# A two-block network on one core: expert e of the routed layer always in block e, six weight slots filled ahead, and the down product one block later

## The reference, cut to what matters

```
expert_id = grp[:, None] * EXPERTS_PER_GROUP + top_e          # 512 tokens x 2 = 1024 assignments
...
def run_block(args):
    xb, e, wb = args
    a = jax.nn.silu(xb @ w_gate[e]) * (xb @ w_up[e])           # 1024 -> 256, twice
    return (a @ w_down[e]) * wb[:, None].astype(xb.dtype)      # 256 -> 1024
```

## Time and profile before

| | |
|---|---|
| median of 3 runs | 1865.17 us (1861.14 to 1869.01) |
| the profiled execution, own time | 1860.19 us |
| its span | 1858.3 us |
| PE busy | 1615.7 us (87%) |
| DVE, POOL, ACT busy | 840.0, 499.6, 450.7 us |
| moved by DMA | 274.97 MB, mean 148 GB/s |
| mean granted TensorE clock | 0.927 of 2.4 GHz |

### The profile page before, as it was taken

One profiled execution on the slowest core, in us unless ns is written; L12 is line 12 of the kernel. 1 busy time (PEld: TensorE's weight loads), 2 busy tenths in 40 slices (PEclk: granted clock), 3 DMA queues, 4 the chain that ended last, 5 costly groups with the idle time before them and its releaser, 6 DMA issues.

```text
span 1858.3 us, 25135 instructions
## 1 busy us (share of the span) xinstructions
PE 1615.7 (87%) x9839; PEld 1303.2 (70%) x9839; DVE 840.0 (45%) x1469; ACT 450.7 (24%) x702; POOL 499.6 (27%) x208
## 2 busy tenths in 40 slices
PE   6967999998999999979999899899998578778782
PEld 5956676697989898958998787655888344444440
DVE  2344545528888884249208502464132523223234
ACT  4211232414222222233323323332232100000001
POOL 2450211123444443323432243200332011101103
PEclk9977999899999999979999999899999579998986
DMA  5161101032444452313221122200230399999994
GB/s 204 69 254 63 46 26 43 11 126 92 187 174 185 178 202 82 107 46 114 101 88 46 46 91 93 96 1 4 101 127 34 117 356 372 374 369 375 379 377 162
DMA packets 41435, 274.97 MB, mean 148 GB/s; under 512 B 5248, under 2 KB 5760, under 8 KB 17536
## 3 DMA queue, kind: packets, MB, share of 16 engines
q1 hardware_dynamic: 31872, 251.13, 36.1%
q0 software_dynamic: 4032, 13.63, 2.3%
q10 hardware_dynamic: 5440, 8.92, 1.3%
HBM read 250.07 MB, written 23.59 MB: 147 GB/s over the span
## 4 chain that ended last, share of the span: by engine, by line
PE 72%; DMA 13%; DVE 9%; ACT 3%; issue 2%; POOL 1%; ACTq 0%; SPq 0%; POOLq 0%; DVEq 0%
PE G L1719 18%; PE G L1721 17%; PE G L1720 17%; DMA wgu<-in_wexp_dram 9%; PE SA L1844 2%; PE SA L2200 2%; DMA arena<-in_wexp_dram 2%; PE G L1741 2%; PE OB L1863 2%; PE G L2200 1%; PE SA L2088 1%; PE PB L1853 1%; PE OB L2104 1%; PE OB L2215 1%; PE SA L2087 1%
## 5 line engine op out<-in xcount | busy, mean ns | idle before, releaser
L596 POOL TENSOR_TENSOR wl<-raw,wh 128x2048 fp32r<-128x2048 f32 x91 | 422.1, 4639 | 832.4 <-ACT wh L709 832.4
L709 ACT ACTIVATE wh<-raw 128x2048 fp32r<-128x2048 f32 x91 | 173.9, 1911 | 275.4 <-PE G L1721 273.2
L1719 PE MATMUL G<-Hh,wh 128*128 128x512 f32 x544 | 220.7, 406 | 4.7 <-DVE Yl L1526 1.6
L1719 PE MATMUL G<-wh,Yh 128*128 128x256 f32 (+2 forms) x700 | 206.3, 295 | 13.4 <-DVE arena L1463 7.3
L1721 PE MATMUL G<-Hh,wl 128*128 128x512 f32 x544 | 213.9, 393 | 0.0
L1720 PE MATMUL G<-Hl,wh 128*128 128x512 f32 x544 | 213.7, 393 | 0.0
L1721 PE MATMUL G<-wh,Yl 128*128 128x256 f32 (+2 forms) x700 | 204.3, 292 | 0.0
L1720 PE MATMUL G<-wl,Yh 128*128 128x256 f32 (+2 forms) x700 | 204.1, 292 | 0.0
L1719 PE MATMUL G<-wh,Hh 128*128 128x256 f32 x640 | 187.4, 293 | 2.6 <-DVE Hl L1530 2.1
L1720 PE MATMUL G<-wl,Hh 128*128 128x256 f32 x640 | 182.6, 285 | 0.0
L1721 PE MATMUL G<-wh,Hl 128*128 128x256 f32 x640 | 182.6, 285 | 0.0
(11 more groups left out here) (367 smaller groups left out, 2391.3 us busy)
## 6 DMA issues: line engine op xcount, KB each, us to landing
raw<-in_pieces_dram SPq DMA_DIRECT2D x91, 1024.0 KB, 4.9
arena<-in_wexp_dram SPq DMA_DIRECT2D x18, 2048.0 KB, 35.0
wgu<-in_wexp_dram SPq DMA_DIRECT2D x16, 2048.0 KB, 34.8
arena<-in_pieces_dram SPq DMA_DIRECT2D x24, 1024.0 KB, 4.8
arena<-in_wexp_dram SPq DMA_DIRECT2D x18, 1024.0 KB, 33.2
wdn<-in_wexp_dram SPq DMA_DIRECT2D x16, 1024.0 KB, 33.7
y_rows<-yb ACTq DMA_DIRECT2D x68, 128.0 KB, 8.9
y_rows<-arena SPq DMA_DIRECT2D x4, 2048.0 KB, 17.9
```

The lines of the kernel that those rows point to most:

```text
L596: pool.tensor_tensor(wl[:, split_slot(s)], wait_raw(pool, p), wh[:, split_slot(s)].bitcast(F32), ALU.subtract).then_inc(S("low_split"), 1)
L709: act.activation(wh[:, split_slot(s)], wait_raw(act, sp_list[s]), ACT.Copy).then_inc(S("high_split"), 1)
L1719: pe.matmul(out, ah, bh, start=first, stop=False)
```

## The change

1. **Order of blocks.** Block e (0 to 31) is always expert e, full or not. An expert's rows beyond 64 go to overflow blocks 32 and up (`OVER` = 16 at most), and only these stay in a loop with table and `If`. The first 32 blocks are written out on every engine. For the inputs here 34 blocks hold rows before; after, there are 32 and two overflow blocks.
2. **Weights.** Six slots in place of four. They are in memory that the earlier stages give up one after the other, and SP fills them as each is free: expert 0 ahead of piece `ga` 2, expert 1 and down of 2 behind the last piece, gate/up of 2 and 3 when the last `wout` product is done, the rest behind the store of `xn_rows` and the routing product. From then on gate/up of b+6 waits for `up_ready` of block b, down of b+6 for `y_ready` of b.
3. **Order on PE.** Down of b-1 follows gate/up of b. Rows are gathered four blocks ahead and turned two ahead. All four XT, GU, AB and YB banks alternate as before.
4. **Small things.** Routing has four more DVE operations (own block's first row). POOL uses the table directly for the first blocks, without a copy of the index. `final_g` is loaded later, in a slot. Two fills of `y_rows` in the first block's attention fall away (two of four 2 MB transfers).

The diff, cut to its core:

```
-NBLK = 48
-MIN_BLK = 2 * T // BS
+OVER = 16
+NBLK = NE + OVER
+AHEAD = 4
+NSLOT = 6
...
-        wgu = [AR(0, 2 * PIECE), AR(2 * PIECE, 2 * PIECE), wgu2[:, :], wgu3[:, :]]
-        wdn = [AR(4 * PIECE, PIECE), AR(5 * PIECE, PIECE), wdn2[:, :], wdn3[:, :]]
+        wgu = [AR(3 * PIECE, 2 * PIECE), gu_y[:, :], gu_w[0][:, :], gu_w[1][:, :], AR(PIECE, 2 * PIECE), gu_h[:, :]]
+        wdn = [AR(5 * PIECE, PIECE), dn_y[0][:, :], dn_y[1][:, :], AR(0, PIECE), dn_h[:, :], dn_l[:, :]]
...
+                if p == ("ga", 2):
+
+                    sp.wait_ge(S("scores_ready"), A0 + len(aunits))
+                    sp.wait_ge(S("score_biased"), A0 + len(aunits))
+                    expert_gu(0)
+                    expert_dn(0)
...
-            sp.dma_start(tab3, tab3_d).then_inc(S("tab3_loaded"), 16)
+            sp.dma_start(tab3, tab3_d[:, 0:TAB3_N]).then_inc(S("tab3_loaded"), 16)
+            expert_gu(1)
+            expert_dn(1)
+            expert_dn(2)
+            wait_group(sp, "wout", 7)
+            expert_gu(2)
+            expert_gu(3)
             sp.wait_ge(S("rows_normed"), 4 * NT)
             sp.dma_start(xn_rows.rearrange("(t p) n -> p t n", p=P), hraw3).then_inc(S("xn_stored"), 16)
             sp.wait_ge(S("xn_stored"), 16)
+            wait_group(sp, "h3", KT - 1)
+            wait_freed(sp, "wout", 7)
+            expert_gu(4)
+            expert_dn(3)
+            wait_group(sp, "gr", 0)
+            expert_dn(4)
+            expert_gu(5)
+            expert_dn(5)
+            for b in range(NE - NSLOT):
+                sp.wait_ge(S("up_ready"), b + 1)
+                expert_gu(b + NSLOT)
+                sp.wait_ge(S("y_ready"), b + 1)
+                expert_dn(b + NSLOT)
...
+            own(dve.tensor_tensor(own64, cols(tab3, TAB3, "iota_b")[:, 0:NE], ps64, ALU.subtract))
+            own(dve.tensor_scalar(Tmp, Sl, float(BS), None, ALU.is_lt))
+            own(dve.tensor_tensor(Tmp, Tmp, own64.unsqueeze(1).to_broadcast([P, NT, 32]), ALU.mult))
+            own(dve.tensor_tensor(Sl, Sl, Tmp, ALU.add))
...
+            for b in range(NE):
+                if b >= 2:
+                    dve.wait_ge(S("act_turned"), b - 1)
+                gated(b, b % 2)
+                scale_shift(b + 2, b % 2)
+                if b >= 1:
+                    row_out(b - 1)
...
+            def turn_and_down(b):
+
+                pe.wait_ge(S("act_whole"), b + 1)
+                if b >= 2:
+                    pe.wait_ge(S("act_copied"), b - 1)
+                act_turned(b % 2, pe.transpose)
+                if b + 3 < NE + 2:
+                    rows_of(b + 3)
+                pe.wait_ge(S(f"down_loaded{b % NSLOT}"), slot_count(b))
+                pe.wait_ge(S("act_copied"), b + 1)
+                if b >= 2:
+                    pe.wait_ge(S("y_copied"), b - 1)
+                down(b, b % 2, b % NSLOT)
...
+            rows_of(0)
+            rows_of(1)
+            for b in range(NE):
+                pe.wait_ge(S("xgT_ready"), b + 1)
+                pe.wait_ge(S(f"gu_loaded{b % NSLOT}"), slot_count(b))
+                if b >= 2:
+                    pe.wait_ge(S("act_whole"), b - 1)
+                gate_up(b, b % 2, b % NSLOT)
+                if b == 0:
+                    rows_of(2)
+                else:
+                    turn_and_down(b - 1)
+            turn_and_down(NE - 1)
```

More of the change, by code:

```diff
@@ L993, in _, with turned_copy, store @@
             act.activation(e2, m2, ACT.Exp).then_inc(S("second_exp"), 1)
+            def turned_copy(b):
+                act.wait_ge(S("act_turned"), b + 1)
+                if b >= 2:
+                    act.wait_ge(S("y_ready"), b - 1)
+                act.activation(actf[:, b % 2, :], AB[b % 2][:, 0:2 * BS], ACT.Copy).then_inc(S("act_copied"), 1)
+            def store(b):
+                act.wait_ge(S("y_copied"), b + 1)
+                for half in range(2):
+                    act.dma_start(y_rows[b * BS:(b + 1) * BS, half * 512:(half + 1) * 512], yb[BS * half:BS * half + BS, b % 2, :]).then_inc(S(f"y_stored{b % 2}"), 16)
@@ new lines, in _ @@
+            for b in range(NE):
+                if b >= 1:
+                    turned_copy(b - 1)
+                act.wait_ge(S("up_ready"), b + 1)
+                if b >= 2:
+                    act.wait_ge(S("tanh_free"), b - 1)
+                act.activation(tanhg[:, b % 2, :], GU[b % 2][0:BS, 0:256], ACT.Tanh, scale=0.5).then_inc(S("tanh_ready"), 1)
+                if b >= 2:
+                    store(b - 2)
+            turned_copy(NE - 1)
+            for b in (NE - 2, NE - 1):
+                store(b)
@@ new lines, in _ @@
+            row_out(NE - 1)
+            dve.wait_ge(S("bexp_ready"), 1)
+            blocks = dve.value_load(nblk_i[0:1, :], min_val=0, max_val=OVER)
+            with dve.Fori(0, OVER // WS) as i:
+                for v in range(WS):
+                    b, u = NE + WS * i + v, v % 2
+                    with dve.If(WS * i + v < blocks):
+                        dve.wait_ge(S("act_turned"), b - 1)
+                        gated(b, u)
+                        scale_shift(b + 2, u)
+                        dve.wait_ge(S("y_ready"), b + 1)
+                        dve.wait_ge(S(f"y_stored{u}"), 32 * (NE // 2) + 64 * i + 32 * (v // 2))
@@ L2169, in _, with gate_up @@
             pe.wait_ge(S("slot_idx_ready"), 1)
[L2172 to L2179 removed]
+            def gate_up(b, u, s):
+                wg = wgu[s].rearrange("p (j k n) -> p j k n", j=2, k=KT)
+                for k in range(KT):
+                    for j in range(2):
+                        ins = pe.matmul(GU[u][BS * j:BS * j + BS, 0:256], xgT[:, u, k, :], wg[:, j, k, :], start=k == 0, stop=k == KT - 1)
+                ins.then_inc(S("up_ready"), 1)
@@ L2180, in rows_transposed, with down, rows_turned @@
+            def down(b, u, s):
+                wd = wdn[s].rearrange("p (k n) -> p k n", k=2)
+                for k in range(2):
+                    for half in range(2):
+                        ins = pe.matmul(YB[u][BS * half:BS * half + BS, :], actf[:, u, k * BS:(k + 1) * BS], wd[:, k, half * 512:(half + 1) * 512],
+                                        start=k == 0, stop=k == 1)
+                ins.then_inc(S("y_ready"), 1)
+            def rows_turned(u, v, first):
                 for k in range(KT):
@@ L2211, in _ @@
-                        pe.wait_ge(S("act_copied"), b + 5)
-                        pe.wait_ge(S("y_copied"), b + 3)
-                        for k in range(2):
-                            for half in range(2):
-                                ins = pe.matmul(YB[u][BS * half:BS * half + BS, :], actf[:, u, k * BS:(k + 1) * BS], wd[:, k, half * 512:(half + 1) * 512],
-                                                start=k == 0, stop=k == 1)
-                        ins.then_inc(S("y_ready"), 1)
+                        pe.wait_ge(S(f"gu_loaded{s}"), before + 16 * i + 16)
@@ L2221, in _kxn @@
+                        pe.wait_ge(S("act_copied"), b + 1)
+                        pe.wait_ge(S("y_copied"), b - 1)
+                        down(b, u, s)
 def _kxn(w):
```

213 lines of the change are left out of this document (117 added, 96 removed).

## The result

The changed kernel took 1818.97 us (median of 4, 1814.19 to 1821.06) beside 1863.16 us (4 runs, 1858.84 to 1869.01) for the kernel before: ratio 0.976 [0.972, 0.979], 44 us faster. The profiled execution took 1820.64 us, 39.6 less than the profiled one of before and 8 less than the 1828.7 that the sum gave for it. So the direction and the place of the gain were right, and the size was not: the time lies 3 us under the range's low end.

What follows compares the result with a forecast made beforehand. DMA bytes at 374 GB/s were taken as the bound: 1498 + 281 + 3.5 = 1782.5 against 1814, so 31.5 us off 1860.2 gives 1828.7. The median forecast was 1831, range 1822 to 1845 (8 in 10).

Steps and rivals of the forecast that it cites:

- the sum: Whole kernel, profiled execution: 1860.2 us before, less 31.5 us for the earlier end of DMA, gives 1828.7.
- the rate of the full queue: Expert stage after the restart: 105.1 million bytes at the old kernel's 374 GB/s take 281.0 us; bounds 372 to 377.
- the restart: Start of expert blocks: expert 6's gate/up weights issued at 1496.7, transfer starting by 1498; bounds 1495 to 1500.
- the hole: After the restart, engines idle some 3.5 us while down weights of expert 6 wait for block 0; bounds 0 and 7.
- sixth step: In the chain to the restart: block 0's gathered rows land at 1487.2, 4.7 us after the gather at 1482.5.
- The tail: After the end of DMA: unchanged, since overflow blocks run in the old order with the same gathers and norm.
- Rival A: Expert stage: DMA stays the bound and about 31 us go; chance 0.79.
- B: Expert stage: PE becomes the bound through its lower clock, from 8.6 us a block; chance 0.07, of which 0.02 slower.
- D: Straight expert blocks: instructions arrive late, gain 12 or kernel 57 us slower; sign: idle PE without releaser; chance 0.05.
- the first 15 blocks or so: Sign of being right: PE has no wait for weights in these expert blocks, then one in each.
- C: Ahead of and entering the experts: piece `ga` 2 or `xn_rows` comes late, gain 15 to 25 us; chance 0.06.
- E: Expert stage: the queue is slower than before, at 356 GB/s, gain 17 us; chance 0.03.

Runs made afterwards that it cites:

- e7: Kernel before the change, with each gather held back by one added POOL wait until stores start, same bytes: 1851.99 us, ratio 0.995 to before.
- e13: Changed kernel with eight idle POOL products ahead of each gather of blocks 4 to 31, so it is issued after the stores: 1826.16 us, ratio 0.984.
- e4: Changed kernel with gathers of blocks 4 to 31 fetching 2 rows in place of 64: 1780.58 us, ratio 0.957 to the kernel before.
- e6: Changed kernel with a third result buffer for block 31 alone, run without the changed kernel beside it: 1815.65 us, ratio 0.977.
- e10: Changed kernel with gathers issued two blocks at a time and a third result buffer for block 31: 1820.15 us, ratio 0.979.
- e11: Same kernel as e6, run beside the changed kernel on one chip: 1815.58 us, ratio 0.975 to the kernel before.
- e3: Changed kernel with no expert loaded early; the six are issued when the block table is ready: 1856.02 us, ratio 0.999.
- e2: Changed kernel with the old order within a block, down and stores directly behind gate/up of the same block: 1818.71 us, ratio 0.979.
- e8: Changed kernel run again unaltered, as base on another chip: 1825.35 us, ratio 0.981 to the kernel before.
- e5: Kernel before the change with loop gathers of blocks 2 and up fetching 2 rows in place of 64: 1835.41 us, ratio 0.986.

## Why the prediction was wrong in size

**The failed step is the rate of the full queue.** "105.1 million bytes, 281.0 us" took 374 GB/s over from the old kernel, and I bounded it at 372 to 377. It measured 389 over 1510 to 1760, and the three profiled executions of the changed kernel have 384 to 389. From the restart (1494.96 and the 1.3 us that I had put behind the issue, so 1496.3; the first packet starts at 1495.93) to the end at 1769.3, less some 0.5 of hole, it is 272.5 us for the same bytes (the trace has 105.4 million), 8.5 less. The unchanged bytes, queue and share were no ground to keep it: the change moved the gathers to the stores, and the diff and a timeline of any later block would have told me to look at when the two are issued. That moving the gather to the stores raises the rate is shown by e7, without a byte changed: up by 20 GB/s and 9 us of time, clear of noise. e13, the way back, has the rate 6 GB/s lower and the time not clear of noise, so it agrees and proves little. e4 shows what gathers cost at all. e7 also moved the gather against the weight transfers, and why a gather costs less beside a store is not settled.

**The restart and the hole.** 1.7 and about 3 us early. The chain was right to its sixth step (rows there at 1487.1, forecast 1487.2). Its products were sized too long: 5.04, 3.67 and 1.94 us where I took 6.4, 4.5 and 3. The upper of the two clock levels is granted from 1492.7 on, behind 2.8 us of gate/up at the lower one, and nothing waits between the products.

**The tail "is the same"** was wrong by 5 us the other way. I followed the overflow blocks, which keep the old order, and not the last straight blocks, whose stores now come two blocks late. e6, e10 and e11 take that wait away, and their ends are some 3 to 8 us shorter in the traces, which is about these 5.

Together: 1.7 + 3 + 8.5 - 5.1 = 8.1 us, the whole difference between 1828.7 and 1820.6. The median is 12 under the forecast 1831: these 8, the 2.3 that I had put on the sum because the median of before stood above its profiled execution, and 1.7 by which the median of the changed kernel stands under its own. The range ended at 38 us of gain, and here a sum was off too: its own bounds (restart 1495, no hole, 105.1 million bytes at 377) give an end at 1773.8, 40 us of gain, and 24.5 at the other end. With 40 the profiled execution, 39.6 faster, lies just inside, but by luck: the longer tail hides 5 us of what the rate gave. The rate, the largest term, was bounded at 377 by rows of one kernel alone; with 384 to 389 the range would have held the result.

**What held.** The early transfers are issued as the order showed and cost nothing that can be told from the runs (`xn_rows` goes at 1440.98, 1.7 us later than before, but in e3, without them, it goes at 1442.18). Rival A was the case: share 1.02 in the stage, and the byte count with the rate of 389 gives an end at 1496.3 + 0.5 + 270.2 = 1767.0, 2 us before the one measured, since it ran slower at first (264 GB/s from 1500 to 1505). PE's block is 6.1 us at the upper level and 9.4 us are there for it (3.67 million bytes at 389), so B was farther off than I thought, though the clock of the 250 us is 0.89. The waits of PE in them:

```profile
PE SA L2280 <- issue: 27.4, 8, 3.7
PE G L2280 <- issue: 8.3, 3, 3.6
PE SA L2280 <- DVE arena L1745: 4.8, 2, 3.4
```

"issue" without a releaser was my sign for D, code that comes late, and 12 instruction packets fell into these 250 us. But e4 has the same straight code with 14 such packets, and its rows for the same 250 us are

```profile
PE SA L2284 <- issue: 3.9, 3, 1.9
PE G L2284 <- issue: 3.4, 1, 3.4
```

With less in the queue 28 of 36 us go away. The packets settle it: from block 11 to block 31 every gate/up of the changed kernel starts 0.5 to 1.1 us after the end of the last packet of its weights, so these waits are for weights whose landing the profile does not name, and D did not happen. (Up to block 10 the weights are in before PE asks for them; I had forecast that for the first 15 blocks or so, and PE catches up sooner, since its block takes 6.1 us.) The Trainium skill (Runtime: NRT & Kernel Launch, Instruction fetch mechanics) had it so for straight code, and the traces agree: 12 packets, 0.3% of the engines' time. C neither: ACT took up piece `ga` 2 at 1328.93, behind an operation that waited for PE, not for a transfer. E was wrong in its sign. The 358 GB/s of the Trainium skill (Perfetto Trace Analysis, Engine Utilization) was no bound to use here: the same section calls it a core's share when both cores of a pair are active, and says that a core alone can pull more. The traces agree: this kernel has one core, and its long stages ran at 374 to 421.

## To carry to other kernels

Where a queue is full, its rate belongs to the mix that flies at one time, not to the bytes: cut the old trace into steps with and without gathers before taking its mean over, and look in the diff for what the change makes meet. Gathers beside a full queue are dear (e4: 28 of them, 41 to 45 us, of which 18 are bytes), and where they can't be saved, try to issue them with the stores; here that was worth 9 us (e7). A result that is stored one block later can need one buffer more where the pipeline drains; the steady part hides it, the handover does not.

## What the runs showed of the hardware

- A gather of 64 rows of 4 KB beside weight transfers brings the 16 engines' 420 GB/s down to some 313 to 326 (before, e2, e13) at a share of 1.0 that stays; two stores of 64 x 2 KB rows leave 410 to 421. In e3 the stretches with gathers alone, four of them ahead at the start, have 260 to 302.
- Turning products that read partitions 0 to 63 and partitions 64 to 127 start in the same 10 ns and run side by side (1505.21 and 1505.21 above).
- The changed kernel's PE clock is 0.89 in the stage, where many of its waits are 3 to 3.7 us long and the gate/up behind such a wait takes 5.4 to 6.5 us in place of 3.67. e2 has 0.98 with waits of 3.0 us at most, e4 0.99 (1510 to 1730) with few. But the length of the waits does not order the clocks: the kernel before has 0.92 with no wait over 2.1 us, e8 also 0.92 with waits up to 4.1 us, and e5 0.88 to 0.89 with none over 1.1 us and none for a transfer. The Trainium skill (TensorE: Matmul & The Clock Gate, HAM oscillation) has gaps from DMA waits lower the clock; the traces agree in part: the drops of the changed kernel stand at such waits, those of e5 cannot. No run here changed the gaps alone. I had used this rule as speaking against B, since the change makes the gaps fewer; it also makes them longer.
